# Gated delta rule: the first four doubling levels of the inverse on four 32 by 32 diagonal blocks instead of on the full 128 by 128 matrices

## The reference

```python
a_mat = jnp.where(strict, jnp.einsum("bhncd,bhnsd->bhncs", k_beta, k) * decay, 0.0)
eye = jnp.eye(CHUNK, dtype=q.dtype)
t_mat = lax.linalg.triangular_solve(eye + a_mat, jnp.broadcast_to(eye, a_mat.shape),
                                    left_side=True, lower=True)
u = jnp.einsum("bhncs,bhnse->bhnce", t_mat, v * beta[..., None])
w = jnp.einsum("bhncs,bhnsd->bhncd", t_mat, k_beta * jnp.exp(g)[..., None])
# per chunk: v_new = u - w S;  o = q_dec S + qk v_new;  S = S g_tot + k_dec^T v_new
```

## Time and profile before

| | us |
|---|---|
| median of 3 runs | 4083.28 |
| the profiled execution | 4082.2 |
| its span in the trace | 4080.4 |
| PE busy | 4033.1 (99%) |
| DVE busy | 2005.5 (49%) |
| POOL busy | 1884.5 (46%) |
| ACT busy | 1456.9 (36%) |

### The profile page before, as it was taken

The page is one execution under the profiler, slowest core; times in us unless marked ns, Lnnn a source line. Parts: engine busy times, 40 slices in busy tenths (PEclk is TensorE's granted clock), DMA queues, the critical chain, the costliest instruction groups (busy, mean ns, idle before and its releaser), DMA issues.

```text
span 4080.4 us, 52747 instructions
## 1 busy us (share of the span) xinstructions
PE 4033.1 (99%) x19360; PEld 3337.6 (82%) x19360; DVE 2005.5 (49%) x3477; ACT 1456.9 (36%) x2200; POOL 1884.5 (46%) x1408
## 2 busy tenths in 40 slices
PE   9999999999999999999999999999999999999998
PEld 7888778888888877888777888888888888888887
DVE  3212553221320354321248663598888836666653
ACT  3223243222322324322334433333677732222222
POOL 4444334444444434444433544455333345555553
PEclk9999999999999999999999999999999999999999
DMA  3222222222222212222222103233455575555542
GB/s 139 97 96 102 73 73 93 93 103 93 93 102 93 97 72 83 93 93 103 99 73 42 33 22 115 104 140 139 165 206 206 206 247 201 190 186 205 190 161 81
DMA packets 144612, 489.65 MB, mean 120 GB/s; under 512 B 17120, under 2 KB 82912, under 8 KB 101984
## 3 DMA queue, kind: packets, MB, share of 16 engines
q1 hardware_dynamic: 49392, 351.29, 24.3%
q10 hardware_dynamic: 95088, 136.56, 9.8%
HBM read 420.68 MB, written 67.14 MB: 120 GB/s over the span
## 4 chain that ended last, share of the span: by engine, by line
PE 44%; issue 32%; POOL 21%; DVE 3%; ACT 0%; POOLq 0%; ACTq 0%; DVEq 0%
POOL w_lo L475 21%; PE bank L1195 13%; PE bank L1196 13%; PE bank L1197 13%; PE bank L2031 1%; PE bank L1774 1%; PE bank L1793 1%; PE bank L1802 1%; DVE gk L2450 0%; DVE gq L2450 0%; PE bank L1966 0%; DVE p_t L2461 0%; DVE a_t L2587 0%; DVE p_t L2464 0%; PE bank L1737 0%
## 5 line engine op out<-in xcount | busy, mean ns | idle before, releaser
L475 POOL TENSOR_TENSOR w_lo<-raw,w_hi 128x512 fp32r<-128x512 f32 x1324 | 1783.0, 1379 | 2088.1 <-ACT w_hi L583 2061.3
L1195 PE MATMUL bank<-h_hi,w_hi 128*128 128x512 f32 x3232 | 1272.4, 394 | 12.8 <-DVE h_lo L2160 9.8
L1196 PE MATMUL bank<-h_lo,w_hi 128*128 128x512 f32 x3232 | 1260.1, 390 | 0.0
L1197 PE MATMUL bank<-h_hi,w_lo 128*128 128x512 f32 x3232 | 1259.5, 390 | 0.0
L583 ACT ACTIVATE w_hi<-raw 128x2048 fp32r<-128x2048 f32 x331 | 632.9, 1912 | 1028.5 <-PE bank L1197 981.2
L1195 PEld LDWEIGHTS bank<-h_hi,w_hi 128*128 128x128 f32 x3232 | 608.1, 188 | 144.3 <-POOL w_lo L475 11.2
L1197 PEld LDWEIGHTS bank<-h_hi,w_lo 128*128 128x128 f32 x3232 | 607.6, 188 | 127.9
L1196 PEld LDWEIGHTS bank<-h_lo,w_hi 128*128 128x128 f32 x3232 | 608.2, 188 | 125.7 <-issue 3.4
L1195 PE MATMUL bank<-w_mix_hi,w_hi 128*128 128x512 f32 x1024 | 398.4, 389 | 0.9 <-ACT stage L998 0.9
L1196 PE MATMUL bank<-w_mix_lo,w_hi 128*128 128x512 f32 x1024 | 398.3, 389 | 0.0
L1197 PE MATMUL bank<-w_mix_hi,w_lo 128*128 128x512 f32 x1024 | 398.3, 389 | 0.0
(11 more groups left out here) (392 smaller groups left out, 4402.1 us busy)
## 6 DMA issues: line engine op xcount, KB each, us to landing
raw<-weights SPq DMA_DIRECT2D x331, 1024.0 KB, 4.8
g_store<-g_buf ACTq DMA_DIRECT2D x8, 4096.0 KB, 18.3
g_in<-g_store ACTq DMA_DIRECT2D x32, 1024.0 KB, 5.5
s_store<-stage ACTq DMA_DIRECT2D x60, 512.0 KB, 2.9
s_in<-s_store ACTq DMA_DIRECT2D x30, 1024.0 KB, 7.5
x<-x_in SPq DMA_DIRECT2D x4, 512.0 KB, 7.9
out<-x SPq DMA_DIRECT2D x8, 256.0 KB, 2.2
q_mask<-rows ACTq DMA_DIRECT2D x6, 256.0 KB, 4.3
```

The costliest lines, as they stand in the source:

```text
L475: pool.tensor_tensor(w_lo[:, slot, cols], raw[:, slot, cols], w_hi[:, slot, cols].bitcast(F32), ALU.subtract).then_inc(lo_written, 1)
L1195: pe.matmul(out_ap, w_hi[:, slot, cols], m_hi, start=start, stop=False)
L1196: pe.matmul(out_ap, w_hi[:, slot, cols], m_lo, start=False, stop=False)
L1197: return pe.matmul(out_ap, w_lo[:, slot, cols], m_hi, start=False, stop=stop)
```

## The change

Levels 1 to 4 work on the diagonal blocks alone. Four new buffers of 32 columns for each head lie in what was `b_t`: `a_small`, `b_small`, `inv_small` and `inv_t_small`. Partition p of them holds row p of its own diagonal block, so the four blocks of a head stand below each other in 32 columns, and a step over all heads has 128 columns instead of 512.

- POOL's `start_inverse` copies the four diagonal blocks of `a_t` to `a_small` (four copies of 32 partitions), and does its multiply and its subtraction on 128 columns. It now also waits for the `inv_t` update of level 5 of the step before. The masks of levels 2 to 4 have 128 columns; those of levels 5 and 6 are gone (PE reads the blocks of `a_t` itself).
- PE's products and updates of levels 1 to 4, and `turn_inverse`, become matmuls of 32 by 32, four blocks for each of four heads: 16 instead of 4.
- ACT's copies and DVE's subtractions in these levels have 128 columns.
- After level 4 the blocks have to stand in the full matrices: ACT writes `inv` (four copies for each direction, behind its copies of level 5), POOL writes `inv_t` (four for each direction, ahead of `triangle` of step n + 1). DVE clears the full matrices once, at n = 0, after levels 1 to 3 (two memsets of 512 columns each time).
- At level 5 DVE writes minus the product where it subtracted before; level 6 is as before.

The diff, with the one-line hunks left out that name two counters anew, and the one by which ACT's fetch of `a_t` for step n waits for PE's product of level 6 (`level_y`) instead of POOL's last mask:

```diff
--- before.py
+++ after.py
@@ -119,2 +119,3 @@
 BLOCK_LEVEL = 5
+EDGE = 1 << BLOCK_LEVEL
@@ -264,2 +265,5 @@
         b_t = [place(f"b_t{n}", [P, GH, P], F32, at=w_hi_at + idle + (2 + n) * GH * P * 4) for n in range(2)]
+        b_small, a_small, inv_small, inv_t_small = ([b[:, :, EDGE * part:EDGE * part + EDGE] for b in b_t]
+                                                    for part in range(4))
+        prod_small = [y[:, :, 0:EDGE] for y in prod_y]
@@ -418,2 +422,18 @@
+        def masked_at(n, level, j):
+
+            return 2 * (BLOCK_LEVEL - 1) * n + 2 * (level - 1) + j + 1
+
+        def diagonal():
+
+            return [slice(at, at + EDGE) for at in range(0, P, EDGE)]
+
+        def small_bank(n):
+
+            return banks[n][:, 0:GH * EDGE].rearrange("p (h t) -> p h t", h=GH)
+
+        def in_small(h):
+
+            return slice(h * EDGE, (h + 1) * EDGE)
+
...
@@ -505,2 +525,5 @@
+            def over_heads_small(m2):
+                return m2[:, None, :].to_broadcast([P, GH, EDGE])
+
@@ -508,5 +531,10 @@
                 pool.wait_ge(sem("a_steps"), a_step(n, 1, j))
-                t = inv_t[n % 2][j]
-                c_it.step(pool.tensor_tensor(t[:, :, :], a_t[n % 2][j][:, :, :], over_heads(masks2[:, 2, :]), ALU.mult))
-                c_it.up(pool.tensor_tensor(t[:, :, :], over_heads(ident), t[:, :, :], ALU.subtract))
+                if n > 0:
+                    pool.wait_ge(sem("inv_written"), inv_t_at(n - 1, BLOCK_LEVEL, j))
+                for d in diagonal():
+                    ins = pool.tensor_copy(a_small[j][d, :, :], a_t[n % 2][j][d, :, d])
+                c_it.step(ins)
+                t = inv_t_small[j]
+                c_it.step(pool.tensor_tensor(t, a_small[j], over_heads_small(masks2[:, 8, 0:EDGE]), ALU.mult))
+                c_it.step(pool.tensor_tensor(t, over_heads_small(masks2[:, 8, EDGE:2 * EDGE]), t, ALU.subtract))
@@ -517,5 +545,5 @@
                 elif n > 0:
-                    pool.wait_ge(sem("level_y"), level_at(n - 1, 6, j))
-                c_lm.up(pool.tensor_tensor(b_t[j][:, :, :], a_t[n % 2][j][:, :, :], over_heads(masks2[:, 2 + level, :]),
-                                           ALU.mult))
+                    pool.wait_ge(sem("level_y"), level_at(n - 1, BLOCK_LEVEL - 1, j))
+                c_lm.up(pool.tensor_tensor(b_small[j], a_small[j],
+                                           over_heads_small(masks2[:, 7, EDGE * (level - 1):EDGE * level]), ALU.mult))
@@ -531,8 +559,13 @@
                 for n in range(4):
-                    for level in range(2, 7):
-                        if level == 6 and n < 3:
-                            for j in range(2):
-                                triangle(n + 1, j)
+                    for level in range(2, BLOCK_LEVEL):
                         for j in range(2):
                             mask_level(n, level, j)
+                    for j in range(2):
+                        pool.wait_ge(sem("inv_written"), inv_t_at(n, BLOCK_LEVEL - 1, j))
+                        for d in diagonal():
+                            ins = pool.tensor_copy(inv_t[n % 2][j][d, :, d], inv_t_small[j][d, :, :])
+                        c_it.step(ins)
+                    if n < 3:
+                        for j in range(2):
+                            triangle(n + 1, j)
...
@@ -839,3 +872,3 @@
                         act.wait_ge(sem("a_turned"), 2 * n + j + 1)
-                        c_is.up(act.activation(inv[j][:, :, :], bank4(side_bank(n, j, FIRST_INVERSE)), ACT.Copy))
+                        c_is.up(act.activation(inv_small[j], small_bank(side_bank(n, j, FIRST_INVERSE)), ACT.Copy))
...
@@ -897,3 +930,3 @@
                             if level < BLOCK_LEVEL:
-                                ins = act.activation(prod_y[j][:, :, :], bank4(4 * j), ACT.Copy)
+                                ins = act.activation(prod_small[j], small_bank(4 * j), ACT.Copy)
@@ -902,2 +935,8 @@
                             c_y.up(ins)
+                        if level == BLOCK_LEVEL:
+                            for j in range(2):
+                                act.wait_ge(sem("inv_written"), inv_at(n, BLOCK_LEVEL - 1, j))
+                                for d in diagonal():
+                                    ins = act.activation(inv[j][d, :, d], inv_small[j][d, :, :], ACT.Copy)
+                                c_is.up(ins)
@@ -1755,3 +1794,3 @@
                 def turn_inverse(n, j):
-                    pe.wait_ge(sem("inv_t_started"), 2 * (2 * n + j + 1))
+                    pe.wait_ge(sem("inv_t_in_place"), 8 * n + 3 * (j + 1))
@@ -1760,3 +1799,4 @@
                     for h in range(GH):
-                        ins = pe.transpose(bank[:, h * P:h * P + P], inv_t[n % 2][j][:, h, :], ident)
+                        for d in diagonal():
+                            ins = pe.matmul(bank[d, in_small(h)], inv_t_small[j][d, h, :], ident[d, d], start=True, stop=True)
@@ -1765,3 +1805,3 @@
                     if level == 1:
-                        pe.wait_ge(sem("inv_started"), 2 * n + j + 1)
+                        pe.wait_ge(sem("inv_in_place"), 4 * n + j + 1)
@@ -1770,10 +1810,15 @@
                         pe.wait_ge(sem("inv_written"), inv_at(n, level - 1, j))
-                    pe.wait_ge(sem("level_masked"), level_at(n, level, j))
+                    if level < BLOCK_LEVEL:
+                        pe.wait_ge(sem("level_masked"), masked_at(n, level, j))
+                    if level == 6:
+                        pe.wait_ge(sem("inv_in_place"), 4 * n + 2 + j + 1)
                     for h in range(GH):
                         if level < BLOCK_LEVEL:
-                            ins = pe.matmul(banks[4 * j][:, h * P:h * P + P], b_t[j][:, h, :], inv[j][:, h, :],
-                                            start=True, stop=True)
+                            for d in diagonal():
+                                ins = pe.matmul(banks[4 * j][d, in_small(h)], b_small[j][d, h, :], inv_small[j][d, h, :],
+                                                start=True, stop=True)
                         else:
                             for r, c in blocks_of(level, j):
-                                ins = pe.matmul(banks[4 * j][r, shifted(c, h)], b_t[j][c, h, r], inv[j][c, h, c],
+                                ins = pe.matmul(banks[4 * j][r, shifted(c, h)], a_t[n % 2][j][c, h, r],
+                                                inv_small[j][c, h, :] if level == BLOCK_LEVEL else inv[j][c, h, c],
@@ -1789,2 +1834,4 @@
                         pe.wait_ge(sem("inv_written"), inv_t_at(n, level - 1, j))
+                    if level == 6:
+                        pe.wait_ge(sem("inv_t_in_place"), 8 * n + 6 + j + 1)
@@ -1792,7 +1839,8 @@
                             if level < BLOCK_LEVEL:
-                                ins = pe.matmul(banks[b + 1][:, h * P:h * P + P], t[:, h, :], prod_y[j][:, h, :],
-                                                start=True, stop=True)
+                                for d in diagonal():
+                                    ins = pe.matmul(banks[b + 1][d, in_small(h)], inv_t_small[j][d, h, :],
+                                                    prod_small[j][d, h, :], start=True, stop=True)
                             else:
                                 for r, c in blocks_of(level, j):
-                                    ins = pe.matmul(banks[b + 1][r, shifted(c, h)], t[r, h, r], prod_y[j][r, h, c],
+                                    ins = pe.matmul(banks[b + 1][r, shifted(c, h)], inv_t_small[j][r, h, :], prod_y[j][r, h, c],
@@ -1801,7 +1849,9 @@
                         if level < BLOCK_LEVEL:
-                            ins = pe.matmul(banks[b + 2][:, h * P:h * P + P], prod_y[j][:, h, :], t[:, h, :],
-                                            start=True, stop=True)
+                            for d in diagonal():
+                                ins = pe.matmul(banks[b + 2][d, in_small(h)], prod_small[j][d, h, :],
+                                                inv_t_small[j][d, h, :], start=True, stop=True)
                         else:
                             for r, c in blocks_of(level, j):
-                                ins = pe.matmul(banks[b + 2][c, shifted(r, h)], prod_y[j][r, h, c], t[r, h, r],
+                                ins = pe.matmul(banks[b + 2][c, shifted(r, h)], prod_y[j][r, h, c],
+                                                inv_t_small[j][r, h, :] if level == BLOCK_LEVEL else t[r, h, r],
@@ -2640,7 +2690,6 @@
                             if level < BLOCK_LEVEL:
-                                ins = dve.tensor_tensor(inv[j][:, :, :], inv[j][:, :, :], bank4(b + 1), ALU.subtract)
+                                ins = dve.tensor_tensor(inv_small[j], inv_small[j], small_bank(b + 1), ALU.subtract)
                             else:
                                 for r, c in blocks_of(level, j):
```

(19 more changed lines are left out.)

6 lines of the change are left out of this document (3 added, 3 removed).

## The result

| | median of the runs, us | ratio to before, 95% interval |
|---|---|---|
| before | 4082.86 (20 runs) | |
| after | 4088.07 (4085.74 to 4094.57, 20 runs) | 1.0015 [1.0009, 1.0022] |

The change makes the kernel slower by 5.2 us. The forecast was 4080, about 3 us faster than before; 4088 lies in the range of 4060 to 4098, but on the other side of the kernel before. The profiled execution of after took 4091.2 us, 3 above its median, so its trace shows a somewhat larger loss.

A forecast was written before the change was run, and what follows sets the result against it. PE was taken to bound levels 1 to 4, DVE and POOL levels 5 and 6. Terms of -25.2, +12.9 and +8.7 us (clock) summed to -3.6, giving 4079.7, called 4080; the range was 4060 to 4098.

The forecast's parts named there:

- What bounds the kernel: Delta rule steps: PE bounds levels 1 to 4, DVE and POOL levels 5 and 6; the change relieves only the first.
- Levels 1 to 4, PE: Cheaper small matmuls, less drains and waits, save 6.3 us a step, 25.2 in four steps.
- rival with halved pitch: Levels 1 to 4: four array positions might halve small matmuls' pitch, 4059; part of the clock-holds rival, chance 0.30.
- What is late next: Level 2: DVE's `inv` update comes late, level takes 5.95 us instead of 7.14, 1.2 less.
- End of level 4 to `new_values`: Chain through POOL and DVE takes 16.1 us for 11.8: 4.3 more a step, 12.9 in all.
- The clock: Small tiles hold the clock worse: 8.7 us in level 3 and 4 of n = 0 and levels 5 and 6.
- the second rival: Levels 2 to 4 of steps 1 to 3: clock stays down, 4.9 us a level, 4099 with four; chance 0.22.
- The sum: Whole kernel: -12.3 us at full clock plus 8.7 of clock gives -3.6 us, forecast 4080.

The follow-up runs named there:

- one weight: Kernel with the triangle first, each group of 16 small matmuls made 4 of head 0's weights by 128 columns (other heads' weights left out); 4053.37 us, 0.9928.
- the triangle first: Kernel after, with POOL's triangle for both directions of the next step put back ahead of the eight copies of inv_t; 4080.28 us, 0.9993.
- looped groups: Kernel with the triangle first, small matmuls of heads 0 to 2 in levels 1 to 4 made a hardware loop over head 0's; 4136.97 us, 1.0137.
- split sides: Kernel with the triangle first, second direction's side group in levels 1 to 4 issued after the updates on PE and DVE; 4071.19 us, 0.9971.
- late turn: Kernel with split sides, turning of the next step's inverse moved behind new_values, second direction's queries in its place; 4063.00 us, 0.9956.

## Why the prediction was wrong

**What bounds the kernel.** "So there are two kinds of place: levels 1 to 4, bound by PE" was right for before and the root of the miss for after. A level has a third limit next to PE and DVE: the instructions that must arrive. By the pace of 3.73 us a packet it lay at 1.9 us a level before (32 large matmuls, 128 instructions, half a packet) and was invisible. After it is 6.1 us.

**Levels 1 to 4, PE (the step that failed).** "Together 6.3 us a step, 25.2 in four steps". Up to the first product of level 5, n = 1 took 33.0 us before and 30.0 after, 3.0 less; n = 3 gains 3.0 too, n = 2 loses 0.4 and n = 0 loses 3.0. That is 2.5 us less in four steps. The term was priced by matmuls and semaphores alone. It was wrong in two parts with opposite signs. The small matmuls of the updates are cheaper than forecast: 0.017 and 0.021 us at full clock and 0.027 to 0.028 at half clock, for 0.036. Those of the product, with 0.023 to 0.027 at full clock, are about the 0.027 forecast. The rival with halved pitch had this in part, since the new groups use four positions and the row of level 5 two; no run isolates the positions. Fetching, which stood in no part of the sum, put 29.1 us of gaps in. The diff said that it was coming: 32 and 64 matmuls where 8 and 16 were, four instructions each.

**What is late next.** DVE was named for level 2. With fetching relieved it is indeed DVE's `inv` update (11.1 us, 19 times, one weight); in the kernel after PE's wait for it is 4.8 us.

**End of level 4 to `new_values`.** Right: 15.6 or 16.4 us, by where it is counted from, for 16.1, and copies 0.29 for 0.33. Levels 5 and 6 of the four steps, `new_values` not counted, took 12.8 us more, for 12.9. The run with the triangle first confirms the part that the order costs, 7.8 us for 3 times 2.6. What I did not draw from my own sum is that this order was a choice and not part of the smaller blocks.

**The clock.** 8.7 us, "the least sure term". The 368 records of large matmuls took 64.5 us; at 1.78 us for 16 they take 41.0, so 23.5 of clock. Before, 1160 records took 137.6 for 129.1, 8.5 of clock. So 15 us more in the large groups alone. The granted clock of the steps, 0.67 to 0.81, is below 0.9 in all of them, so the term was not void; it was too small. And the second rival ("the clock stays down") was closer: its condition, below 0.75 in steps 1 and 2, was met in n = 2 only (0.81 and 0.74). It was lowest in n = 0, as forecast, but it was low in all four steps. The reason given, "small tiles don't hold the clock as large ones do", is not borne out: small tiles without fetch gaps kept 1.00, and the same tiles with fetch gaps fell to 0.61. The looped groups, with a short pause behind every eight records in place of the fetch gaps, had 0.63 to 0.68, so pauses of another kind go with a low clock too. The earlier trace rows has pauses as well as small tiles (PE busy for 2.41 of 3.40 us). n = 1 with one weight, without fetch gaps, has 0.87 for 0.84 with the triangle first. How much of the lost clock in this kernel the fetch gaps cause, and how much the other pauses, stays open.

**The sum.** Forecast for levels 1 to 4: -25.2, and 7.4 of the clock's 8.7, so -17.8. Measured in the profiled executions: -2.5. Forecast for levels 5 and 6: +12.9 and 1.3 of clock, so +14.2; measured +12.8. So the four steps became 10.3 us longer where 3.6 shorter was forecast, and the whole miss is in levels 1 to 4; at the medians it is 8 us. Being near 4080 owed something to chance: cheaper small matmuls and unforeseen fetching went against each other.

## What to carry to other kernels

Count instructions as well as work: where a change replaces one matmul with sixteen small ones, put the instructions of the stretch over the pace at which they arrive (here 256 per 3.73 us, after a reserve of some 500) beside PE's time, and spread them between long instructions. A gap of "issue" in the middle of a group of an engine, ending just behind a packet of the instruction queue, is the sign. When a change moves work between queues, try it in the old order first: the copies ahead of the triangle cost more than the whole loss, and with that order, split sides and a late turn the smaller blocks are 19 us faster than before.
